# A hybrid attention, mixer and expert step: keys and router columns loaded early, the last tiles' norms spaced wider, no empty instructions on TensorE

## The reference, cut to what matters

```python
sh1, sc1, g1, sh2, sc2, g2 = modulation(c, w_ada, b_ada)     # silu(c) @ w_ada + b_ada
h = modulate(rmsnorm(xs, norm_mix), sh1, sc1)
q, k, v, p = split_projection(h, w_in)                       # one product
q, k = apply_axial_rope(q, ...), apply_axial_rope(k, ...)    # sample only
attn = latent_attention(q, k, v, cache_k, cache_v, sink)     # window +-128 and 512 cached keys
mix  = concat([attn, pool_mixer(p, pool_w, pool_scale)]) @ w_out
xs = xs + g1 * mix
h = modulate(rmsnorm(xs, norm_ffn), sh2, sc2)
affin = softmax(h @ w_router)                                # 16 experts
gates, idx = top_k(affin.T, 2 * n / 16)                      # each expert takes 128 (32) tokens
y = (silu(h[idx] @ w_gate) * (h[idx] @ w_up)) @ w_down * gates
xs = xs + g2 * scatter_add(y)
y_sample = rmsnorm(xs, norm_final)
```

## Time and profile before

| | |
|---|---|
| median of 3 runs | 3505.99 us (3499.99 to 3514.11) |
| profiled execution | 3510.94 us |
| its span | 3509.1 us |
| PE busy | 3299.6 us, 94% of the span |
| DVE busy | 2136.6 us, 61% |
| ACT busy | 1758.9 us, 50% |
| POOL busy | 592.0 us, 17% |
| DMA | 776.31 MB, mean 221 GB/s |

### The profile page before, as it was taken

How to read it: one execution, slowest core, us unless ns; L and a number is a source line. 1 busy time by engine, 2 the same in 40 slices (tenths; PEclk the granted TensorE clock), 3 DMA queues, 4 the chain that set the end, 5 groups by cost and what they waited for, 6 DMA issues and landing times.

```text
span 3509.1 us, 52491 instructions
## 1 busy us (share of the span) xinstructions
PE 3299.6 (94%) x21154; PEld 3004.1 (86%) x21154; DVE 2136.6 (61%) x2354; ACT 1758.9 (50%) x1823; POOL 592.0 (17%) x616
## 2 busy tenths in 40 slices
PE   5899999998999999998959999999999999999995
PEld 4677777777788877887759999999999999999995
DVE  5544444354442344234967777777777777777766
ACT  5553543454452255223335555555555555555554
POOL 1046136102321023401110000000000000000101
PEclk9899999999899999998979999999999999999997
DMA  7676565577214421442757988888898888888987
GB/s 268 240 256 225 169 229 195 196 262 248 96 32 155 162 86 33 153 151 98 241 181 234 292 271 279 270 257 264 269 281 278 273 268 258 267 276 277 288 284 290
DMA packets 545054, 776.31 MB, mean 221 GB/s; under 512 B 16240, under 2 KB 409680, under 8 KB 536240
## 3 DMA queue, kind: packets, MB, share of 16 engines
q1 hardware_dynamic: 507072, 616.60, 53.7%
q0 software_dynamic: 37872, 158.16, 13.9%
HBM read 708.51 MB, written 66.19 MB: 221 GB/s over the span
## 4 chain that ended last, share of the span: by engine, by line
PE 81%; DVE 7%; ACT 4%; DMA 4%; issue 3%; POOL 1%; DVEq 0%; ACTq 0%; POOLq 0%; SPq 0%
PE PS L859 30%; PE PS L636 14%; PE PS L861 12%; PE PS L807 11%; PE PS L753 2%; PE PS L732 2%; PE PS L582 2%; DVE wlo L1241 2%; PE PS L583 1%; ACT whi L942 1%; PE PS L741 1%; PE PS L676 1%; PE PS L771 1%; PE PS L869 1%; PE PS L841 1%
## 5 line engine op out<-in xcount | busy, mean ns | idle before, releaser
L859 PE MATMUL PS<-xT,hi_f 128*128 128x320 f32 x4096 | 1060.3, 347 | 3.7 <-DVE hraw L1616 3.7
L1552 DVE TENSOR_TENSOR lo_f<-raw_f,hi_f 128x2048 fp32r<-128x2048 f32 x384 | 879.0, 2289 | 284.0 <-ACT hi_f L1149 283.6
L861 PE MATMUL PS<-xT,lo_f 128*128 128x160 f32 x4096 | 968.2, 236 | 0.0
L1241 DVE TENSOR_TENSOR wlo<-raw,whi 128x2048 fp32r<-128x2048 f32 x204 | 475.2, 2346 | 630.6 <-ACT whi L942 630.2
L1149 ACT ACTIVATE hi_f<-raw_f 128x2048 fp32r<-128x2048 f32 x384 | 734.0, 1911 | 183.7 <-PE PS L861 89.5
L861 PEld LDWEIGHTS PS<-xT,lo_f 128*128 128x128 f32 x4096 | 786.4, 192 | 0.0
L859 PEld LDWEIGHTS PS<-xT,hi_f 128*128 128x128 f32 x4096 | 770.9, 188 | 3.9 <-DVE hraw L1616 3.9
L942 ACT ACTIVATE whi<-raw 128x2048 fp32r<-128x2048 f32 x204 | 387.4, 1915 | 568.6 <-PE PS L807 298.2
L859 PE MATMUL PS<-hid,hi_f 128*128 128x320 f32 x2048 | 536.0, 348 | 9.8 <-DVE yT L1634 9.8
L861 PE MATMUL PS<-hid,lo_f 128*128 128x160 f32 x2048 | 484.2, 236 | 0.0
L859 PEld LDWEIGHTS PS<-hid,hi_f 128*128 128x128 f32 x2048 | 385.4, 188 | 10.5 <-DVE yT L1634 10.5
(11 more groups left out here) (305 smaller groups left out, 4611.9 us busy)
## 6 DMA issues: line engine op xcount, KB each, us to landing
raw_f<-w_gate SPq DMA_DIRECT2D x128, 1024.0 KB, 5.9
raw_f<-w_up SPq DMA_DIRECT2D x128, 1024.0 KB, 5.3
raw_f<-w_down SPq DMA_DIRECT2D x128, 1024.0 KB, 5.7
raw<-w_ada SPq DMA_DIRECT2D x96, 1024.0 KB, 5.2
raw<-w_in SPq DMA_DIRECT2D x60, 1024.0 KB, 5.3
raw<-w_out SPq DMA_DIRECT2D x48, 1024.0 KB, 5.4
arena_ab<-x_sample POOLq DMA_DIRECT2D x8, 1024.0 KB, 12.4
arena_cd<-x_sample POOLq DMA_DIRECT2D x8, 1024.0 KB, 6.5
```

The costliest lines, as they stand in the source:

```text
L859: nc.tensor.matmul(PS[:, b + m, 0:2 * CAP], hi_f[:, n % NSPL_F, r, w], x, start=(kt == 0), stop=False, skip_group_check=True)
L861: ins = nc.tensor.matmul(PS[:, b + m, 0:CAP], lo_f[:, n % NSPL_F, r, w], x[:, 0:CAP], start=False, stop=(kt == last_kt), skip_group_check= ...
L1241: nc.vector.tensor_tensor(wlos[slot(n)], raws[slot(n)], whis[slot(n)].bitcast(F32), ALU.subtract).then_inc(lo_ok, 1)
L1552: nc.vector.tensor_tensor(lo_f[:, n % NSPL_F], raw_f[:, n % NRAW_F], hi_f[:, n % NSPL_F].bitcast(F32), ALU.subtract).then_inc(f_lo_ok, 1)
```

## The change

- `PE_PAD` is an empty tuple: there are no empty instructions at the start of TensorE's program any more.
- `w_router` and `norm_ffn` are loaded at the start, behind the first rows of x, into places of their own (`wr`, `modr`). The keys and the first query rows of chunk 0 are loaded within the projection loop, after the item that completes the last column they need, into `ktm0` and `qq0`. The four modulation rows for the router are issued there too. `kv_in` is divided into `k_in` and `v_in`; values and band are loaded behind the projections.
- In chunk 0 the first mixer unit stands at (0, 2) instead of (0, 0). Its transfers are issued before the first residual rows.
- The router's bias is computed in another form: 16 matmuls of two columns (`router_sums`), a copy, then two matmuls (`router_bias`), placed before the first query unit and one unit behind it.
- The splits of the first two w_out pieces stand within the attention of chunk 0 instead of before it.
- Sample tops are transposed before the last `route`; the sample gather is issued before the prompt's top-k is done, the prompt gather when its indices are there, and the gate tables behind it. The token planes are made in the order of four sample parts, then prompt, with the first low split ahead of the prompt's plane.
- `PAIR_AT` is (8, 16, 18, 20, 22). Norms of tiles 8 and 9 (prompt) stand at the end, behind the scaling of the last expert's rows; three of four row additions stand before the last output column is scaled. GpSimd scatters the sample rows before it stores the two prompt tiles.

The diff, cut:

```diff
...
-PE_PAD = 95
+PE_PAD = ()
...
-MIX_AT = [[(0, 0), (1, 3), (2, 3), (3, 5)], [(0, 0), (0, 4), (1, 0), (1, 5)]]
+MIX_AT = [[(0, 2), (1, 3), (2, 3), (3, 5)], [(0, 0), (1, 3), (2, 3), (3, 5)], [(0, 0), (0, 4), (1, 0), (1, 5)]]
...
-PAIR_AT = (7, 14, 16, 18, 20)
+PAIR_AT = (8, 16, 18, 20, 22)
...
+        ktm0 = arena[0][:, 0:9 * KW].rearrange("p (a b) -> p a b", a=9)
+        ktms = (ktm0, ktm, ktm)
+        qq0 = arena[0][:, 9 * KW:9 * KW + AW]
...
-            for _ in range(PE_PAD):
-                pe.nop().then_inc(pe_pad, 1)
...
+                    pe.wait_ge(k_in, kv_by[tc])
...
+                        ins = nc.tensor.transpose(flat[:, (z % 8) * P:(z % 8 + 1) * P], ktms[tc][:, kb, kv * P:(kv + 1) * P], ident[:])
...
-            pe.wait_ge(col2_ok, 1)
-            for c in range(2):
+
+            def router_sums():
+
+                pe.wait_ge(col2_ok, 1)
                 for kt in range(KT):
-                    last = nc.tensor.matmul(PS[:, 6, c * NE:(c + 1) * NE], s2col[:, c, kt:kt + 1].to_broadcast([P, P]),
-                                            wr[:, kt, :], start=(kt == 0), stop=(kt == KT - 1))
-            last.then_inc(c_tr, 1)
+                    last = nc.tensor.matmul(PS[0:NE, 6, 0:2], wr[:, kt, :], s2col[:, :, kt], start=(kt == 0), stop=(kt == KT - 1))
+                last.then_inc(c_sum, 1)
+
+            def router_bias():
+
+                pe.wait_ge(c_col, 1)
+                for c in range(2):
+                    last = nc.tensor.matmul(PS[:, 6, c * NE:(c + 1) * NE], ccol[:, c:c + 1].to_broadcast([NE, P]),
+                                            ident[0:NE, 0:NE], start=True, stop=True)
+                last.then_inc(c_tr, 1)
+
...
+                        if k == q_unit(0, 0):
+                            router_sums()
+                        if k == q_unit(0, 0) + 1:
+                            router_bias()
...
+                        if hc == heads_by(unit_start[tc]):
+                            pe.wait_ge(v_in, kv_by[tc])
...
+            pe.wait_ge(tops_ok, 1)
+            nc.tensor.transpose(PS[:, 2, 0:NE], top[:, 0:CAP_S], ident[0:NE, 0:NE])
+            nc.tensor.transpose(PS[:, 2, NE:2 * NE], topf[:, 0:CAP_S], ident[0:NE, 0:NE]).then_inc(tops_tr, 1)
...
-            for j in range(4):
-                pe.wait_ge(h_in, j + 2)
-                if j:
-                    pe.wait_ge(x_lo, j)
-                turn_tokens(j)
+            for j in range(5):
+                turn_first(j)
+            pe.wait_ge(x0_lo, 5)
+            nc.tensor.nop().then_inc(x_tr, 4)
...
-            for _ in range(NOUT):
-                split_hi()
...
-                        if tc and gi == 1:
+                        if gi == 1 or tc == 0 and gi == 2:
...
-                act.wait_ge(x_tr, j + 1)
-                take_hi(j)
+                act.wait_ge(x0_tr, j + 1)
+                sample_hi(j).then_inc(x0_hi, 1)
+            act.wait_ge(x0_tr, 5)
+            prompt_hi().then_inc(x0_hi, 1)
+            nc.scalar.nop().then_inc(x_hi, 4)
...
+            for n, c in enumerate((0, 1, 2, 4, 3)):
+                act.wait_ge(e_add, n + 1)
+                if n:
+                    act.wait_ge(e_sq, n)
+                nc.scalar.activation(junk3[:, 0:CC], y_s[:, c * CC:(c + 1) * CC] if c < 4 else y_p[:], ACT.Square,
                                      accum_out=esq[:, c:c + 1]).then_inc(e_sq, 1)
...
+            tile_root(4)
...
+                            if k == 1:
+                                router_columns()
+                                nc.vector.memset(band[:, P:6 * P], 0.0).then_inc(band_ok, 1)
+                            if k == q_unit(0, 0) - 1:
+                                dve.wait_ge(c_sum, 1)
+                                nc.vector.tensor_copy(ccol, PS[0:NE, 6, 0:2]).then_inc(c_col, 1)
+                            if k == q_unit(0, 0):
+                                dve.wait_ge(c_tr, 1)
+                                nc.vector.tensor_copy(cb.rearrange("p a b -> p (a b)"), PS[:, 6, 0:2 * NE]).then_inc(c_ok, 1)
+                                dve.wait_ge(band_ok, 1)
+                                dve.wait_ge(band_in, 32)
...
-                    if tc and j == MIX_AT[cond][1][0] * NH + MIX_AT[cond][1][1] + 2:
+                    if j in [MIX_AT[tc][z][0] * NH + MIX_AT[tc][z][1] + 2 for z in ((1,) if tc else (1, 2))]:
                         split_lo()
...
+                if tc == 2:
+                    nc.vector.tensor_copy(topf[:, 0:CAP_S], topi[:, 0:CAP_S]).then_inc(tops_ok, 1)
...
+            dve.wait_ge(tops_tr, 1)
+            nc.vector.tensor_copy(gate_s[:], PS[:, 2, 0:NE])
+            link(nc.vector.tensor_copy(idx_s[:], PS[:, 2, NE:2 * NE]))
+            nc.vector.tensor_copy(ig_s[:], idx_s[:, 0:1]).then_inc(ig0_ok, 1)
+            dve.wait_ge(tab_in, 16 * (3 + 3 * Q))
+            nc.vector.scalar_tensor_tensor(out=a2_s[:], in0=a2_s[:], scalar=1.0, in1=y_s[:], op0=ALU.add,
+                                           op1=ALU.mult).then_inc(a2_ok, 1)
...
+            nc.vector.memset(yTp[:], 0.0)
+            nc.vector.memset(yT[:], 0.0).then_inc(yT_ok, 8)
...
-            dve.wait_ge(tab_in, 16 * (3 + 3 * Q))
-            link(nc.vector.scalar_tensor_tensor(out=a2_p, in0=a2_p, scalar=1.0, in1=y_p[:], op0=ALU.add, op1=ALU.mult))
-            link(nc.vector.scalar_tensor_tensor(out=a2_s[:], in0=a2_s[:], scalar=1.0, in1=y_s[:], op0=ALU.add, op1=ALU.mult))
+            dve.wait_ge(a2_ok, 2)
+            modulate(1, 16, -1)
+            modulate(2, 16, -1)
+            first_lo(0)
+            modulate(3, 16, -1)
+            first_lo(1)
+            modulate(4, 16, -1)
+            first_lo(2)
+            modulate(0, 16, 4)
+            first_lo(3)
             split_f(0, 0)
-            for j in range(5):
-                modulate(j, 16, 0)
-            nc.vector.memset(yTp[:], 0.0)
-            nc.vector.memset(yT[:], 0.0).then_inc(yT_ok, 8)
-            for j in range(4):
-                take_lo(j)
-                if j < 3:
-                    split_f(j + 1, 0)
+            first_lo(4)
+            nc.vector.nop().then_inc(x_lo, 4)
+            for n in range(1, 4):
+                split_f(n, 0)
             dve.wait_ge(g2_in, 16 * (1 + Q))
...
+                                if not more:
+                                    for z in range(3):
+                                        add_rows(z)
                                 scale_rows(3)
...
-                            tile_norm(TT - 1)
+                            tile_norm(ST - 1)
...
             dve.wait_ge(yp_ok, NE)
-            dve.wait_ge(ys_ok, 4 * NE)
-            dve.wait_ge(gs_in, 16 * (NE + 1))
...
+            add_rows(3)
+            tile_means(4)
...
+            tile_rstd(4)
+            tile_norm(ST)
+            tile_norm(ST + 1)
...
+            for z in range(4):
+                dma(wr[:, 4 * z:4 * z + 4, :],
+                    t["w_router"][0, z * 512:(z + 1) * 512].rearrange("(t p) e -> p t e", p=P)).then_inc(mod_in, 16)
+            dma(modr[4 * KT:5 * KT, :], t["norm_ffn"].rearrange("l (t p) -> (l t) p", p=P)).then_inc(mod_in, 16)
...
+                    if ITEMS[j - 2][1:3] == (2, 2):
+                        pool.wait_ge(h_tr, 3 * KT)
+                        pool.wait_ge(stg_out, 16 * stores_by[12])
+                        load_keys(0)
+                        load_q(0)
+                        mods_stored(20 - ADA_ROWS)
+                        for z in range(4):
+                            dma(modr[z * KT:(z + 1) * KT, :], mod_d[z % 2, (3 + z // 2) * D:(4 + z // 2) * D].rearrange(
+                                "(t p) -> t p", p=P)).then_inc(mod_in, 16)
...
+            pool.wait_ge(used, D0)
+            pool.wait_ge(lo_ok, D0)
+            dma(band[:, 0:P], t["k_mask"][0]).then_inc(band_in, 16)
+            dma(band[:, 6 * P:7 * P], t["k_mask"][1]).then_inc(band_in, 16)
...
+            load_values(0)
...
+            mixer(0, 0)
+            pool.wait_ge(unit_pe, q_unit(0, 0) + 1)
             load_x1(0)
             load_x1(1)
...
+            pool.wait_ge(rs_out, 16 * 2)
+            pool.wait_ge(ig0_ok, 1)
+            gather_s()
             store_rstd(2)
+            free_x1(11)
             pool.wait_ge(rs_out, 16 * (2 + Q))
             pool.wait_ge(gate_ok, 1)
 
...
+            gather_p()
+            gate_tables()
...
-            store_tile(2)
             raw_free(21)
             load_tile(8)
-            store_tile(3)
             raw_free(22)
             load_tile(9)
+            store_tile(2)
...
-            for i in range(4, TT):
+            for i in range(3, ST):
                 store_tile(i)
-            for i in range(TT):
-                pool.wait_ge(f_out[i], 16)
+            pool.wait_ge(fs_out, 16 * (ST - 2))
             pool.wait_ge(ic_ok, NE)
-            pool.wait_ge(e_ok, 2)
+            pool.wait_ge(e_ok, 1)
```

(4 more changed lines are left out.)

182 lines of the change are left out of this document (95 added, 87 removed).

## The result

The changed kernel is slower: 3539.68 us in the median (3530.42 to 3552.69, 5 runs) against 3505.99, a ratio of 1.010 (95% interval 1.007 to 1.013). The forecast was 3488, in a range of 3474 to 3502. The profile is of the run of 3552.69 us, with a span of 3550.9 us; that is 13 us above the median, and I read stages of it, not its sum.

A forecast was written before the change was run, and what follows sets the result against it. TensorE bounds the kernel (81% of the span), with time decided at start, hand-over, gather and tail. Terms 1.0+10.3+12−5 = 18.3 us took the median from 3505.99 to 3487.7, called 3488, range 3474 to 3502.

The forecast's parts named there:

- the loop's term: Expert loop: its 15 passes stay at 102.8 us or so each, with about as few instruction packets.
- R3: Expert loop: its moved place makes each pass fetch instructions again, 1.95 us a pass, 3517 up to 3530; chance 0.06.
- Start: Kernel start: removing empty instructions ahead of PE's first transpose gains 1.0 us, bounds +2 and −2.
- Hand-over: Projections to attention: no transfer waited for, first head at 875.1 against 897.40, gain 22.3 us before the splits' cost.
- the values and band: Hand-over: first heads waiting for values or band transfers, now issued later, would take 2 to 5 us, within the forecast's range.
- Splits: Attention of chunk 0: two w_out splits now inside it cost 12 us, lower bound 7.8.
- Gather: Ahead of the first expert: sample gather before the prompt's selection gains 12 us, range +7 to +14.
- Tail: After the last expert: prompt norms and stores behind the final scaling lose 5 us, range −9 to +1.

The follow-up runs named there:

- 245: Changed kernel with 245 empty instructions put into TensorE's program, 182 of them at the start: 3551.09 us, 1.012 of the kernel before.
- late router: Changed kernel with 120 empty instructions, w_router and norm_ffn transfers moved from the start to behind the first keys and query rows: 3487.21 us, 0.993.
- old end: Changed kernel with 120 empty instructions, old PAIR_AT spacing, prompt tiles normed in the last pass, stores before scatters, early row additions kept: 3480.66 us, 0.991.
- 148: Changed kernel with 148 empty instructions put back (85 at the start, 19 and 44 at later waits): 3486.87 us, 0.994 of the kernel before.
- 95: Changed kernel with 95 empty instructions, 85 at the start and 10 ahead of the wait for the prompt's tops: 3483.70 us, 0.993.
- 120: Changed kernel with 85 + 35 empty instructions, the base of six further runs; not run alone, those runs measured 3479.40 to 3497.98 us.
- 60: Changed kernel with 60 empty instructions at the start of TensorE's program: 3598.23 us, 1.025 of the kernel before.

## Why the prediction was wrong

The failed step is the loop's term. The sum put it at nothing ("15 passes at 102.8 us or so each"), and R3, which named the mechanism, had a chance of 0.06 and a price of 1.95 us a pass. In its place the runs showed 106.80 us a pass and nine packets fetched in each of the 14 passes behind a branch back, 56 us in all; with the loop at its old place 53 us came back. Chance and price were both wrong.

- **The chance.** I argued that 7 packets in 15 passes show that the loop isn't fetched again. They show it for the place before, and I moved the place by 148. I then counted 8 blocks now and 7 after from the program's own instruction numbers, taking a block to begin at a number divisible by 256. The packets' places in the trace (earliest at 256n − 105) say that it doesn't: by them it is 7 before and 8 after, the opposite. What the page of the Trainium skill says ("Runtime: NRT & Kernel Launch", section "Instruction fetch mechanics": 2048 instructions in blocks of 256, a taken branch to a block not held forces a fetch) fits the runs with 7 blocks touched, with no packet in 14 branches back; I fed it with the wrong offset. The same section speaks of a window of two blocks for a branch's target, and the runs with 7 touched don't bear that out. With 8 blocks of 256 the body fits by size, and yet the runs with 8 touched are fetched anew; the block that is asked for ahead of the branch may have to be counted too. That is an estimate from that page, not a measurement.
- **The price.** The nearest row, 1.95 us of issue at the start, was no measure. It was the empty instructions themselves: their records run from 0.84 to 15.22 us without a break. A pass paid 4.0 us: a gap of 2.3 to 3.0, and then, in 7 of 14 passes, half clock for 3.4 or 6.8 us. With the block's end close it was 7.1 to 8.1. R3's sum was off too: two fetches a pass at 1.95 would be 3488 + 58 = 3546, not 3530.
- **Start** (+1.0). The transpose came 2.0 us earlier. Yet at 260 us the pieces stood 7.0 us behind the kernel before in the changed kernel's profile, and in those of the later runs with the change, the one with 245 aside, from 0.3 ahead to 5.6 behind. No run shows why; the late router didn't settle it.
- **Hand-over** (+22.3). 27.8 in the changed kernel's profile, counted from the last modulation row; the sums were 1.02 us, below my lower end of 3.5, because I scaled 16 columns as if the cost hung on the records alone. What I left out is that the early loads delay the last pieces by 3 to 9 us. I had listed the values and band as rivals, not the raw pieces.
- **Splits** (−12). 9.3 us in the changed kernel's profile, some 6.6 in five others, 4.9 to 11.1 in all (7.8 was my lower end). What else made the stretch of chunk 1, with its clock of 0.86, so long wasn't looked for.
- **Gather** (+12). 9.2 to 10.6 in all profiles of the change.
- **Tail** (−5). 4.4 to 4.9 us; the end order is shown as its cause by the run with the old end. Part of the hit is luck. I took −2 for the norm that no longer stands ahead of the last output, but another norm of 4.62 us stands there now (3515.32), and PE's wait for that output fell only from 5.02 us (at 3484.08 in the kernel before) to 4.57 us. From the last output to the end it was 30.5 us, not 31.8.
- **Not forecast.** From the first output projection of chunk 0 to the last of the prompt it is 714 to 719 us in all kernels with the change and 723 to 724 in the two without, 4 to 10 us of gain. No run isolated it; the load of keys and values there is the same, and the mixer's first unit or the earlier bias may be behind it. It stays open.

Without the loop's term the sum is near: a gain of 18.3 us was forecast, and the kernels with 148 and 95 gained 20.9 and 24.1. That is luck in part, since misses cancel. In the profile with 148, against that of before, the projections lost 11.8 us, the hand-over gained 27.2, the splits cost 6.6, the rest of the attention and output stages gained 7.7, the gather 9.2 and the last expert 3.0, and the tail lost 4.9: 23.8 in all.

## What to carry to other kernels

Before an edit that adds or removes instructions ahead of a long hardware loop, read the instruction queue over the loop. If few packets move there, the loop isn't fetched again, and its place is an asset that each edit ahead of it can lose; after the edit look at that number first. Empty instructions at a place where the engine waits anyway repaired it here (95, 120 and 148 of them; 60 and 245 didn't), so the right number has to be found by trying. A row that stands for another cause isn't a bound on an unknown price: a stall on the engine that sets the time costs its length and what the clock does behind it.

## What the runs showed of the hardware

- A loop of 1,663 instructions on TensorE is either fetched once (6 or 7 packets of 16 KB in 15 passes) or anew in each pass (133 packets, 9 behind each branch back). In the kernel before, 95 empty instructions far ahead of it make the difference; more of them (245 in the changed kernel) bring the fetching back.
- Fetching anew costs 3.4 to 4.0 us a pass, or 7.1 to 8.1 where the loop begins shortly before a block's end. The engine is idle for 2.2 to 3.0 us behind the branch, and for 0.3 to 3.2 us at the second gap.
- One gap of 2.2 to 3.0 us on a TensorE that was busy throughout is followed by the half clock (1.2 GHz) for 3.4 or 6.8 us in some passes only: 7 of 14 in the changed kernel, 4 of 14 with 245. With two gaps it is all 28 passes of the two kernels, for 6.8 or 10.2 us.
- Empty instructions with a semaphore increment take 0.15 us each, 95 of them 14.4 us: 182 at the start moved the first transpose to 28.77 us, 85 only to 13.94.
